# Every second gate tile of two mixer layers as a three-part split product, its low part made by an accumulating DMA

## The reference

```python
h = modulate(rms_norm_2(x, mixer_norm_g[l]), sh1, sc1)
proj = h @ w_in[l]                      # 1024 -> 3584 columns
u_conv = proj[..., :2 * D_CONV]         # 8 tiles of 128 columns: a
u_pool = proj[..., 2 * D_CONV:2 * D_CONV + D_POOL]        # 4 tiles: p
gate_a, gate_b = jnp.split(jax.nn.sigmoid(proj[..., 2 * D_CONV + D_POOL:]), N_BRANCHES, axis=-1)  # 16 tiles: G
y_a = conformer_conv_branch(u_conv, ...)   # depthwise conv of 31 taps, layer norm, silu, product
y_b = pool_branch(u_pool, ...)             # window means, grouped product
mixed = gate_a * y_a + gate_b * y_b
x = x + g1[:, None, :] * (mixed @ w_out[l])
```

## Time and profile before

| | |
|---|---|
| three executions | 1587.14, 1584.29, 1581.72 us |
| the profiled execution, its own time | 1583.49 us |
| its span in the trace | 1581.8 us |
| mean granted TensorE clock | 0.954 of full speed |
| PE busy | 1455.4 us (92%) |
| DVE busy | 907.0 us (57%) |
| ACT busy | 578.3 us (37%) |
| GpSimd busy | 3.7 us (9 instructions) |
| HBM read | 416.71 MB, 265 GB/s over the span |

### The profile page before, as it was taken

One profiled execution on the slowest core, in us unless ns is written; L12 is line 12 of the kernel. 1 busy time (PEld: TensorE's weight loads), 2 busy tenths in 40 slices (PEclk: granted clock), 3 DMA queues, 4 the chain that ended last, 5 costly groups with the idle time before them and its releaser, 6 DMA issues.

```text
span 1581.8 us, 26922 instructions
## 1 busy us (share of the span) xinstructions
PE 1455.4 (92%) x10563; PEld 1179.7 (75%) x10578; DVE 907.0 (57%) x1609; ACT 578.3 (37%) x916; POOL 3.7 (0%) x9
## 2 busy tenths in 40 slices
PE   9999999989888899999999999988779999997786
PEld 7999999989877798999998899432217989532223
DVE  6898877684434466888877986310006997410002
ACT  5543456523445554443345154221116144321101
POOL 0000000000000000000000000000000000000000
PEclk8999999999989999999999999999989999999996
DMA  8998844413422344888874659899996749799995
GB/s 319 381 356 309 304 163 158 146 44 107 187 67 94 107 147 174 312 301 304 307 264 169 222 191 363 334 409 409 409 409 252 278 134 366 278 409 409 409 409 232
DMA packets 115803, 420.87 MB, mean 266 GB/s; under 512 B 12944, under 2 KB 13088, under 8 KB 115568
## 3 DMA queue, kind: packets, MB, share of 16 engines
q1 hardware_dynamic: 114624, 414.19, 70.3%
q0 software_dynamic: 1072, 5.20, 0.9%
HBM read 416.71 MB, written 2.62 MB: 265 GB/s over the span
## 4 chain that ended last, share of the span: by engine, by line
PE 68%; DMA 14%; DVE 6%; SPq 5%; ACT 4%; issue 3%; DVEq 0%; ACTq 0%
PE work L934 26%; PE acc L934 12%; PE work L969 7%; PE work L1025 5%; SPq L753 5%; DMA raw<-wstream_d 3%; PE work L1571 3%; DMA over_splits<-wstream_d 3%; DMA over_end<-wstream_d 2%; DMA hf<-wstream_d 2%; PE work L904 2%; PE work L894 2%; ACT whi L1661 1%; PE work L1506 1%; PE work L1598 1%
## 5 line engine op out<-in xcount | busy, mean ns | idle before, releaser
L2115 DVE TENSOR_TENSOR wlo<-raw,whi 128x1024 fp32r<-128x1024 f32 x264 | 321.1, 1223 | 176.0 <-ACT whi L1661 175.3
L1661 ACT ACTIVATE whi<-raw 128x1024 fp32r<-128x1024 f32 x264 | 277.3, 1057 | 278.7 <-PE work L934 189.3
L934 PE MATMUL work<-hhi,whi 128*128 128x256 f32 x1024 | 294.0, 287 | 2.2 <-DVE hlo L2143 1.3
L934 PE MATMUL work<-hlo,whi 128*128 128x256 f32 x1024 | 292.6, 286 | 0.0
L934 PE MATMUL work<-hhi,wlo 128*128 128x256 f32 x1024 | 292.5, 286 | 0.0
L934 PEld LDWEIGHTS work<-hhi,whi 128*128 128x128 f32 x1024 | 199.5, 195 | 4.6 <-DVE wlo L2115 2.5
L934 PEld LDWEIGHTS work<-hlo,whi 128*128 128x128 f32 x1024 | 199.6, 195 | 0.1
L934 PEld LDWEIGHTS work<-hhi,wlo 128*128 128x128 f32 x1024 | 199.5, 195 | 0.0
L2886 DVE TENSOR_TENSOR pair_b<-work,pair_a 128x256 f32<-128x256 f32 x16 | 6.8, 425 | 216.8 <-ACT pair_a L2068 216.8
L2226 DVE SCALAR_TENSOR_TENSOR ada_tiles<-ada_tiles,c_act 128x1024 f32<-128x1024 f32 x96 | 116.3, 1220 | 1.8 <-DMA ada_tiles<-ada_d 1.8
L969 PE MATMUL work<-hf,raw 128*128 128x256 f32 x512 | 111.5, 379 | 0.0
(11 more groups left out here) (494 smaller groups left out, 2708.8 us busy)
## 6 DMA issues: line engine op xcount, KB each, us to landing
raw<-wstream_d SPq DMA_DIRECT2D x376, 512.0 KB, 4.8
ada_tiles<-ada_d SPq DMA_DIRECT2D x96, 512.0 KB, 5.1
over_splits<-wstream_d SPq DMA_DIRECT2D x80, 512.0 KB, 15.1
over_select<-wstream_d SPq DMA_DIRECT2D x48, 512.0 KB, 14.2
over_end<-wstream_d SPq DMA_DIRECT2D x24, 512.0 KB, 14.7
spare_d<-wstream_d SPq DMA_DIRECT2D x24, 512.0 KB, 14.4
over_pool<-wstream_d SPq DMA_DIRECT2D x22, 512.0 KB, 15.2
hf<-wstream_d SPq DMA_DIRECT2D x20, 512.0 KB, 14.8
```

What stands on the lines that cost most here:

```text
L934: mm = pe.matmul(out, a, b, start=(start and k == 0), stop=(stop and k == n - 1), skip_group_check=skip)
L1661: act.activation(whi[n % AHEAD][:], tiles[SLOT[SPLITS[n]]][:], ACT.Copy).then_inc(s("hi_done"), 1)
L2115: dve.tensor_tensor(wlo[n % AHEAD][:], tiles[SLOT[SPLITS[n]]][:], whi[n % AHEAD][:].bitcast(F32), ALU.subtract).then_inc(s("lo_done"), 1)
```

## The change

Every odd gate tile becomes a split tile. ACT makes its high part, and then writes the negated high part into the low buffer (`negated`: a copy with scale -1.0, which rounds in the same way). GpSimd then issues a DMA from the raw tile to the low buffer which adds to what is there, waits until it has landed, and counts it in `lo_done`; so raw minus high stands in the low buffer without DVE. ACT does high and negated part of G1 and G3 ahead of taking out p2 and p3, and those of G5 to G15 ahead of taking out G1, G3, ... G11. The two sums between the gate tiles move by one tile, from after 10 and 11 to after 11 and 12. DVE waits for the eighth DMA of the layer before it splits the pool tile, so that `lo_done` counts in order.

```diff
@@ stream
-        out += [(f"G{l}", m, False) for m in range(16)]
+        out += [(f"G{l}", m, m % 2 == 1) for m in range(16)]
@@ SHARED
-                            ("dn_osq", 1), ("dn_oroot", 1)]),
+                            ("dn_osq", 1), ("dn_oroot", 1), ("negated", 8 * LAYERS)]),
+    **shared("rows_stored", [("rows_stored", 16), ("rest_landed", 16 * 8 * LAYERS)]),
@@
-LN_MEAN_G, LN_VAR_G, SPLIT_G = 10, 11, 16 - AHEAD
+LN_MEAN_G, LN_VAR_G, SPLIT_G = 11, 12, 16 - AHEAD
@@ GpSimd
             for l in range(LAYERS):
+                pool.wait_ge(s("lo_done"), NUMBER[START[f"G{l}"] + 1])
+                for j in range(8):
+                    n = NUMBER[START[f"G{l}"] + 2 * j + 1]
+                    pool.wait_ge(s("hi_done"), n + 1)
+                    pool.wait_ge(s("negated"), after("negated", 8 * l + j + 1))
+                    pool.dma_start(wlo[n % AHEAD][:], tiles[SLOT[SPLITS[n]]][:], accum_op=ALU.add
+                                   ).then_inc(s("rest_landed"), 16)
+                    pool.wait_ge(s("rest_landed"), after("rest_landed", 16 * (8 * l + j + 1)))
+                    pool.nop().then_inc(s("lo_done"), 1)
                 pool.wait_ge(s("flag_ready"), after("flag_ready", l + 1))
@@ ScalarE
+            def negated(n):
+
+                act.activation(wlo[n % AHEAD][:], tiles[SLOT[SPLITS[n]]][:], ACT.Copy, scale=-1.0
+                               ).then_inc(s("negated"), 1)
+
@@ ScalarE
                 for m in range(4):
+                    if m >= 2:
+                        n = NUMBER[START[f"G{l}"] + 2 * m - 3]
+                        hi(n)
+                        negated(n)
                     evac(START[f"p{l}"] + m, ppad[:, m, 16:16 + T], m % 4)
                 for m in range(16):
+                    if m % 2 == 1 and m < 12:
+                        n = NUMBER[START[f"G{l}"] + m + 4]
+                        hi(n)
+                        negated(n)
                     evac(START[f"G{l}"] + m, gate2[:, m, :], m % 4, ACT.Sigmoid)
@@ VectorE
                 pooling(3).then_inc(s("pooled"), 1)
+                dve.wait_ge(s("lo_done"), NUMBER[START[f"pool{l}"]])
                 for m in range(SPLIT_G, 16):
                     lo(NUMBER[START[f"pool{l}"]] + m - SPLIT_G)
```

## The result

The changed kernel took 1603.73 us (median of 4 runs, 1597.0 to 1607.12) against 1584.4 us: ratio 1.0117, 95% interval 1.0078 to 1.0155. The forecast was 1580.0 us with a range up to 1592. The profiled execution took 1602.1 us, its span is 1600.1 us, 18.3 us more than the span of before.

The account below looks back on a forecast made before the run. PE was taken to bound the changed stage. Per layer, 4.60 us from shorter tiles less 2.65 us of bank waits, twice, gives 3.9 us less: 1580.0 us, range 1575.5 to 1592.

Parts of the forecast that it names:

- What bounds, and the tiles: Gate stage: PE alone sets the chain; an unsplit tile takes 3.454 us, a split one 2.879, saving 4.60 us per layer.
- The two bank waits: PE waits 1.8 us ahead of G12 and 0.85 us ahead of G13 for DVE to read the sums' banks, 2.65 us together.
- The adding DMA: GpSimd's add for each odd gate tile lands 5.5 us after issue, ahead of PE's need, and costs nothing.
- 16 x 1.3 us or twice that, where they are half idle: DMA engine time that the sixteen adds occupy, in stretches where the engines were taken as half idle.
- SP waits in order for it: nothing.: SP's load queue waits for an odd tile's add to free the raw buffer, behind loads waiting for PE anyway; no cost.
- From one add to the next: GpSimd's queue in the gate stage: 0.1 us was added to each add's time from issue to landing.
- my limit of 6.3 us: Longest add, issue to landing, that costs nothing up to G11; above it the delay is 6 (L - 6.3).
- Rival 1: Adds slower than 6.3 us set the gate stage's pace, G5 to G11 waiting; gain gone at 6.6 us, 1600 at 8; chance 0.25.
- VectorE holding up GpSimd's issue: DVE's taps might delay each add's issue by one tap, 0.42 us; expected not to, and still within 6.3 us.
- Behind the stage: After the gate stage, through router and experts: the 1.95 us gained per layer carries on to the end in full.
- The 1.3 us of cover for the pool tile: End of the gate stage: DVE's chain has the pool tile's low part ready 1.3 us ahead of PE.
- The same pieces to 0.01 us: The second layer's chain in the changed stretches was read as having the first layer's pieces, equal to 0.01 us.

## Why the prediction was wrong

- **What bounds, and the tiles.** The tiles are right, 3.46 and 2.87 us in turn. That PE goes on setting the stage held only from G4 on in the first layer and from G8 on in the second; ahead of that the adds did.
- **The two bank waits.** Right in place and size: 1.71 and 0.84 us against 1.8 and 0.85, shown alone by the moved sums and removed by the other banks.
- **The adding DMA, "I take 5.5 us, and no cost".** This is the step that failed, and it cost 8.19 + 10.81 = 19.0 us in the two stages. I took one duration for all adds, from a 1 MB load issued at a DMA share of 0.69, and asked whether that was under 6.3 us. It held for the second half of each layer (4.5 to 5.5 us) and not for the first (7.1 to 11.1, apart from 6.1 and 5.6 for G5 and G7 of the first layer). What I left out is an account of engine time. In the 6.33 us of two gate tiles there are two raw loads, and with the raw loads up to G8's, which go out while PE is at G2, two early ones: 4 x 1.4 = 5.6 us, and an add of 3.0 makes 8.6. Without the early loads it is 5.8 of 6.33, which fits but leaves an add beside loads for most of its time. The account is not the whole: with the early loads sent earlier, adds still took 6.4 to 9.2 us, and the trace's stages were still 13.0 us over. I had written "16 x 1.3 us or twice that, where they are half idle"; the twice was right, half idle was the average over a stretch of which the first part stood at 0.77.
- **"SP waits in order for it: nothing."** Wrong in a way I did not look for, and by the stages the larger part: the wait for an odd tile's buffer now ends with its add, soon after the end of the even tile ahead of it or before that, and SP sent tiles in pairs. Spacing them again gave back about 9 us by the ratios, and 8.2 in the stages.
- **From one add to the next** I took 0.1 us. The chain of the version with spaced loads shows 881.83 - (874.72 + 6.46) = 0.65 us. At 5.5 us an add this alone brings the period to 6.15 of the 6.33 us there are, so that my limit of 6.3 us was really about 5.7.
- **Rival 1** named the mechanism, the tiles G5 to G11 and a limit of 6.6 us. It came at G1, G3 and, in the second layer, G7. There the four adds from 1254.02 to 1288.3 were each issued 0.6 to 0.7 us after the one before had landed, so G7 waited for their sum, which is the pace that the rival speaks of. In the versions with the early loads moved the chain runs through five and six adds in a row. I gave it 0.25.
- **VectorE holding up GpSimd's issue** is no rival here: over 897 to 912 DVE was busy for 15.00 of 15 us, and three adds were issued in 2.51 us, 0.84 each, as long as when DVE was idle.
- **The clock.** After PE's wait of 5.2 us ahead of G3 the tile took 4.64 us, 1.77 more, and the granted clock of the stretch 897 to 912 was 0.90: for part of it PE ran at the lower of the two levels, 1.2 GHz. I had no term for it; a tile of that length came three times in the two layers.
- **Behind the stage.** The traces agree with one to one, as I had it, within -3.1 to +6.4 us, and so does the run with 24 idle matmuls; the medians of several other versions moved by some 4 us more than their stages, which stays open. The 1.3 us of cover for the pool tile held too: its low part was ready at 945.49, PE began it at 946.90.
- **A reading.** "The same pieces to 0.01 us" holds from G0 on; a0 to p3 took 35.01 us in the second layer, not 34.55. Nothing in the sum rests on it.

## What to carry to other kernels

A DMA that is hidden by time must also be paid in engine time: add up what every stream takes of the DMA engines in the period that the new one has, part of the stage by part, before asking for its latency. That the sum fits is not enough when loads go out together just ahead of it. When a buffer comes free earlier, ask what the queue behind it will now send at once. And count the gap between one DMA and the next in its period. A sum moved by one tile in a rotation of banks must be checked against the bank of the tile that now follows it.

## What the runs showed of the hardware

An accumulating DMA of 512 KB within SBUF took 4.5 to 4.8 us from issue to landing at its shortest, a copy of the same 2.9 to 3.0; of the 16 engines' time they took 3.0 and 1.5 us, a load of the same size from HBM 1.4. Issuing took 0.83 to 0.92 us on GpSimd for the add and 0.53 for the copy, and a landing was followed by the next issue after 0.65 us. With four loads of 512 KB sent just ahead of it and two more while it ran, the add took 11.1 us. At a DMA share of 0.99 with two loads sent 1.2 us behind it, it took 5.5.
